# Mixer row projections: two of 512 columns in place of four of 256, with the recurrence's key transposes ahead of the values' projection

## The chip, the cores and the metric

The kernel runs on one core of a Trainium2 chip. The metric is the device time of one execution in microseconds; the time before is 2207.61 us, the median of three runs. Engines are called as in the profile: PE (TensorE), DVE (VectorE), ACT (ScalarE), POOL (GpSimd), SP (SyncE, which here only issues DMAs).

## What is computed

Two blocks follow each other on one sequence of 512 tokens and 1024 channels. The change touches the first, which has two layers, each with a mixer and a feed-forward part. The mixer, cut to what matters here:

```
h = rms_norm(x, attn_norm_w[layer]);  proj = h @ w_in[layer]          # 1024 -> 3072
a_q, a_i, a_zf, a_zb, a_g, b_u, c_q, c_k, c_v = jnp.split(proj, ...)  # 6 x 256, 3 x 512
o_a = hgrn2_mixer(a_q, a_i, a_zf, a_zb, a_g, lb)   # gated recurrence, both directions; a_i: its values
o_b = fourier_mixer(b_u)                           # 2-D DFT, over positions and channels
o_c = dilated_attention_mixer(c_q, c_k, c_v, positions)   # rotary on q and k, then attention
x = x + concatenate([o_a, o_b, o_c]) @ w_out[layer]
x = x + square(relu(rms_norm(x, ...) @ w_up)) @ w_down
```

## The kernel before

All weights are split into a rounded part and a remainder, so one product of a tile takes three matmuls: high by high, low by high, high by low. A **chunk** of weights (128 x 2048 words) comes by a DMA from SP into one of two buffers `raw`; ACT casts each half into `WH` (`act_hi`, the cast), DVE makes the remainder `WL` (`dve_lo`), and that half is a **unit** for PE. Three unit buffers exist. SP issues a load once the chunk two before it is split (`sp_chunk`).

Most projections (`pe_lin`) hold the weights still and stream 512 tokens of `HH`/`HL`; their result has channels on the partitions. Four **row projections** of 256 columns per layer need tokens on the partitions: `a_i` (the recurrence's values), `b_u`, and `c_v` in two halves. `pe_rows` holds 128 tokens still and streams 256 columns of weights. ACT empties each result from PSUM, scaled by the norm (`act_made`).

Each engine's program is written as generators woven by a string of letters. In a mixer `u` is a step of the projections (a quarter of one: `u1` to `u48` here), `c` a step of the recurrence; the strings are `MIX_PE`, `MIX_DVE` and `MIX` (ACT and POOL). An engine executes what it is given in that order. The projections stand in the order gates (two), `a_q`, `a_g`, `a_i`, then `c_q` (two halves), `c_k` (two), `b_u`, `c_v` (two). Steps for the next split are two `u` ahead of a chunk's half: at `u38` the first half of chunk 10 is split, at `u42` that of chunk 11.

The recurrence has eight score levels (l = -1 to 6), two `c` each: PE multiplies keys by queries in 128 x 128 blocks (16 matmuls), DVE merges them. Between levels DVE makes the exponents (`apart`), ACT takes `Exp`, POOL and DVE the scaled keys and queries (`queries`). The level -1 starts after `u16` and every level has three `u`, so **level 6** starts after `u37`. After it, in `rec_pe`, come the **key transposes** (four sets of four blocks of 128 x 128), the state's products, the outputs, a sum and its inverse spread over heads (the inverse's broadcast). The sets of the transposes, like all products of the recurrence, go round three PSUM banks (`REC`), and a bank is taken again when its reader is done:

```
                    b = bank()                 # rec_pe: waits for the reader of three sets ago
                        t = e.tr(b[:, ch * 128:(ch + 1) * 128], x.kl[dr][...], ident)
                    e.act(x.Kt[dr]..., t3(b, 4), ACT.Copy)     # rec_act: reads one set
```

So the fourth set's bank is free once ACT has copied the first set.

Rotary turns `c_q` and `c_k`, eight pieces i of 128 x 512. SP swaps each piece's halves by four DMAs into one of two buffers (`sp_turn`), which may start when piece i-2 is finished; POOL multiplies by the cosine, DVE by the sine (`rot_dve`, step i) and, in the next step, adds (piece i-1 finished). `ROT` sets the steps: step i stands two `u` after step i-1. SP's program has, for each of these four projections, the swaps of its two pieces behind the load of the chunk three later:

```
                sp_chunk(e, n)
                if n - 3 in lin_of_chunk and lin_of_chunk[n - 3] in turned_lins:
                    sp_turn(e, lin_of_chunk[n - 3])
```

Behind the projections stand the DFT (`four_pe`, two parts) and the attention.

Of the kernel before, what the change touches and what calls it, by code (L numbers as in the profile page):

```python
# [12 lines left out]
ACT = mybir.ActivationFunctionType  # L13
# [3 lines left out]
S = 512  # L17
# [32 lines left out]
class Book:  # L50
# [17 lines left out]
    def at(self, name, *key):  # L68

        return (self.handle(name), 0) if self.counting else (self.handles[name], self.values[name, key])  # L70
# [150 lines left out]
def build(nc, I, out):  # L221
    ctx = ExitStack()
    with ctx:
# [61 lines left out]
        rcol = small[:, 232:236]  # L285
# [19 lines left out]
        def lin(src, kind, to=None, j=0, ly=0):  # L305
            lins.append(Lin(len(lins), [chunk(x) for x in src], kind, to, j, ly))
            return lins[-1]
# [4 lines left out]
        def unit(u):  # L312
            cs = slice(u % NUNIT * UNIT, (u % NUNIT + 1) * UNIT)
            return WH[:, cs], WL[:, cs]
# [6 lines left out]
        def mix_memory(ly):  # L321
            m = Mix()
# [36 lines left out]
            m.ms, m.rs, m.ris = (small[:, 256 + 32 * i:288 + 32 * i] for i in range(3))  # L359
            W = I["w_in"][ly]  # L360
            m.head = [lin([W[2, 0]], "gate", j=0, ly=ly), lin([W[3, 0]], "gate", j=1, ly=ly),
                      lin([W[0, 0]], "silu", m.aq2, ly=ly), lin([W[4, 0]], "silu", m.ag2, ly=ly),
                      lin([W[1, 0]], "rows", m.ai3, ly=ly)]
            m.tail = [lin([W[6 + j, 0]], "copy", m.cq3[:, 2 * j:2 * j + 2], ly=ly) for j in range(2)]
            m.tail += [lin([W[8 + j, 0]], "copy", m.ck3[:, 2 * j:2 * j + 2], ly=ly) for j in range(2)]
            m.tail += [lin([W[5, 0]], "rows", m.u3, ly=ly)]
            m.tail += [lin([W[10 + j, 0]], "rows", m.cv3[:, :, 256 * j:256 * j + 256], ly=ly) for j in range(2)]
            m.dft = chunk(I["dft"], "raw")
            m.out = [lin([I["w_out"][ly][j, 0]], "res", (m.scratch, 2 * ly), j, ly) for j in range(4)]
            f = m.ffn = Mix()  # L370
# [127 lines left out]

        BANK, BEFORE, holder = {}, {}, {}
        for l in lins:  # L500
            for m in range(2):
                b = (2 * (l.n - s2.low[0].n) + m) % 3 if l.kind in ("lat", "shift", "keep") else l.n % 2 * 2 + m
                BANK[l.n, m], BEFORE[l.n, m] = b, holder.get(b)
                holder[b] = (l, m)

        def bank_of(l, m):
            return bk(BANK[l.n, m])

        def clear(e, l, m):

            if BEFORE[l.n, m]:
                e.wait_ge(*emptied(*BEFORE[l.n, m]))

        def emptied(l, m):

            return at("lin_act" if l.kind in ("rows", "copy") else "lin_dve", "ps", l.n, m)
# [23 lines left out]
        def pe_lin(e, l):  # L540
            for ci, n in enumerate(l.chunks):
                u0 = chunks[n][2]
                for h in range(2):
# [4 lines left out]
                    for m in range(2):  # L548
# [15 lines left out]
                            t.then_inc(*did("w_use", u))  # L564
                        yield

        def pe_rows(e, l):

            u0 = chunks[l.chunks[0]][2]
            for h in range(2):  # L570
                e.wait_ge(*at("w_lo", u0 + h))
                wh, wl = unit(u0 + h)
                for m in range(2):
                    if h == 0:
                        clear(e, l, m)
                    for tk in (2 * m, 2 * m + 1):
                        o = bank_of(l, m)[:, tk % 2 * 256:(tk % 2 + 1) * 256]
                        for k in range(4):
                            xh, xl, made = operand(l, h * 4 + k)
                            e.wait_ge(*at(*made))  # L580
                            xh, xl = xh[:, tk * 128:(tk + 1) * 128], xl[:, tk * 128:(tk + 1) * 128]
                            ws = slice(k * 256, (k + 1) * 256)
                            e.mm(o, xh, wh[:, ws], h + k + tk % 2 == 0, False)
                            e.mm(o, xl, wh[:, ws], False, False)
                            t = e.mm(o, xh, wl[:, ws], False, h + k + tk % 2 == 5)
                    if h:
                        t.then_inc(*did("lin_mm", l.n, m))
                    elif m:
                        t.then_inc(*did("w_use", u0))
                    yield  # L590

        def pe_lins(e, ls):
            for l in ls:
# [1 line left out]

        def act_made(e, l):

            for m in range(2):
                ps = bank_of(l, m)
                if l.kind in ("gate", "silu"):  # L600
                    sg = mixes[l.ly].sg[m]
                    e.wait_ge(*at("lin_dve", "ps", l.n, m))
                    if l.kind == "silu":
                        p = lins[l.n - 1]
                        e.wait_ge(*at("lin_dve", "sg" if p.kind == "gate" else "out", p.n, m))
                    e.act(sg, sg if l.kind == "gate" else l.to[:, m, :], ACT.Sigmoid).then_inc(*did("lin_act", "sg", l.n, m))
                elif l.kind == "rows":
                    e.wait_ge(*at("lin_mm", l.n, m))
                    e.wait_ge(*at("nrm_dve", 2 * l.ly - 1, "col"))
                    for i in range(2):  # L610
                        t = e.act(l.to[:, 2 * m + i, :], ps[:, i * 256:(i + 1) * 256], ACT.Copy,
                                  rcol[:, 2 * m + i:2 * m + i + 1])
                    t.then_inc(*did("lin_act", "ps", l.n, m))
                elif l.kind == "copy":
                    e.wait_ge(*at("lin_mm", l.n, m))
                    e.act(l.to[:, m, :], ps, ACT.Copy).then_inc(*did("lin_act", "ps", l.n, m))
                elif l.kind == "keep":
                    e.wait_ge(*at("lin_dve", "ps", l.n, m))
                    e.act(s2.keep[m], s2.keep[m], ACT.Sigmoid).then_inc(*did("lin_act", "keep", l.n, m))
                elif l.kind == "hid":  # L620
                    f, half = l.to
                    t = 2 * l.j + m
                    e.wait_ge(*at("ffn_dve", l.ly, half, "sq", t))
                    e.act(f.hh[:, t, :], f.rl[m], ACT.Copy).then_inc(*did("ffn_act", l.ly, half, "hi", t))
                elif l.kind == "res" and l.to[1] is not None:
                    act_next(e, l, m)
# [281 lines left out]
        def rec_pe(e, x):  # L908
# [32 lines left out]
                        t = e.tr(b[:, ch * 128:(ch + 1) * 128], x.kl[dr][:, (hp * 4 + ch) * 128:(hp * 4 + ch + 1) * 128], ident)  # L941
                    t.then_inc(*did("rec_pe", ly, "kt", dr, hp))
            yield
            e.wait_ge(*at("lin_act", "ps", x.head[4].n, 1))
            for dr in range(2):
                for hp in range(2):
                    e.wait_ge(*at("rec_act", ly, "kt", dr, hp))
# [268 lines left out]
        def four_pe(e, x, first_scores):  # L1216
            ly = x.ly
            n = x.dft
            e.wait_ge(*at(f"raw{n % NRAW}", n))
            e.wait_ge(*at("fou_dve", ly, "folded"))  # L1220
            for part in range(2):
                w = slot(n)[:, part * 768:(part + 1) * 768]
                for d in range(2):
                    b, ds = bk(part * 2 + d), slice(d * 128, (d + 1) * 128)
                    l = x.tail[-1 if part else -2]
                    e.wait_ge(*emptied(l, 1))
                    e.wait_ge(*emptied(x.tail[-1], 1))
                    e.mm(b[:, 0:128], x.u04[:, ds], w[:, 0:128])
                    e.mm(b[:, 256:384], x.u24[:, ds], w[:, 128:256])
                    for k in range(2):  # L1230
                        t = e.mm(t3(b, 2)[:, :, 128:256], x.uo[:, k, ds], t3(w[:, 256 + k * 256:512 + k * 256], 2), k == 0, k == 1)
                    if part and d:
                        t.then_inc(*did("raw_use", n))
                        mark("raw_use", ly, part, d)
                    else:
                        t.then_inc(*did("raw_use", ly, part, d))
                yield
            e.wait_ge(*at("fou_act", ly, 0, 1))
            next(first_scores)
            for d in range(2):  # L1240
                e.wait_ge(*at("fou_act", ly, 1, d))
                e.mm(bk(2 + d), c("cd"), x.us[d], True, False)
                e.mm(bk(2 + d), c("sd"), x.us[2 + d], False, True).then_inc(*did("fou_pe", ly, d))
            yield
# [26 lines left out]

        ROT = 14

        def turned_of(x, i):

# [196 lines left out]
        def win_dve(e, x):  # L1474
# [17 lines left out]
            for i in range(9):  # L1492
                steps[f"s{ROT + i}"] = lambda i=i: rot_dve(e, x, i)
            for i, also in ((21, fold), (22, fold_again)):
                steps[f"s{i}"] = lambda i=i, also=also: (rot_dve(e, x, i - ROT), also(e, x))
            yield from between(dve_lins(e, x.head + x.tail, True), **steps)
            att = att_dve(e, x.ly, x, full, mask, -0.125, evac)
            yield from four_dve(e, x, att)
# [5 lines left out]
        def win_pool(e, x):  # L1504
            yield from between(range(48), **{f"s{ROT + i}": lambda i=i: rot_pool(e, x, i) for i in range(8)})

        MIX = "u" * 12 + "c" + "uu" + "cucuu" * 8 + "cuu" * 4 + "cuuuc"
        MIX_DVE = "u" * 12 + "c" + "uu" + "cuucu" * 8 + "cuu" * 4 + "cuuuc"
        MIX_PE = "u" * 16 + "c" + "cucuu" * 8 + "cu" * 2 + "cuuu" + "cu" + "cuuuc"

# [1765 lines left out]
def layout(inp):  # L3278
# [6 lines left out]
    a["w_out"] = np.stack([lay(g["w_out"][i], 8, 256) for i in range(2)])  # L3285
    a["w_up"] = np.stack([lay(g["w_up"][i], 8, 256) for i in range(2)])
    a["w_down"] = np.stack([lay(g["w_down"][i], 8, 256) for i in range(2)])
    q = {k[:-2]: x[0] for k, x in g.items() if k.endswith("_2")}
    a["pos2"] = np.ascontiguousarray(g["positions_2"][0])
    w = q["w_in"]  # L3290
# [43 lines left out]
```

## Time and profile before

| What | Value |
|---|---|
| timed runs | 2207.59, 2207.61, 2208.95 us |
| span of the profiled execution | 2211.8 us |
| PE busy | 2148.4 us, 97% of the span |
| DVE / ACT / POOL busy | 1324.7 / 949.9 / 189.1 us |
| chain that ended last | PE 86%, DVE 7%, ACT 3% |
| first mixer's projections and recurrence | 10 to 193 us |
| the same part of the second | begins 639 us later |

The span is what the profiler saw from the first to the last instruction of one execution; a time of its own beside the span was not kept for it. It is 4.2 us above the median of the timed runs, so a difference worked out from its rows is put on the median.

### The profile page before, as it was taken

The page shows a single profiled execution, that of the slowest core. Times are in us where ns is not written, and L with a number is a line of the kernel's source. Part 1 is how long each engine was busy: PE and PEld are TensorE (multiplying, and loading weights), DVE is VectorE, ACT ScalarE, POOL GpSimd, SP SyncE. Part 2 cuts the span into 40 slices and gives each one's busy share as a digit, 9 for nine tenths or more (in the row PEclk, how much of TensorE's full clock was granted, in tenths as well). Part 3 has the DMA queues.
Part 4 walks back from the last instruction along what each step waited for, and adds up shares of the span by engine and source line. Part 5 has one row for each costly group of instructions (what it writes and reads, how often), then busy time and mean ns, then how long its engine had stood idle before and what let it go on. Part 6 is the DMA issues. An engine that isn't in the chain of part 4 may idle for free.

```text
span 2211.8 us, 32932 instructions
## 1 busy us (share of the span) xinstructions
PE 2148.4 (97%) x13984; PEld 1681.6 (76%) x13984; DVE 1324.7 (60%) x1976; ACT 949.9 (43%) x1442; POOL 189.1 (9%) x159
## 2 busy tenths in 40 slices
PE   8998999999999999999999999999999998999997
PEld 6885688888888785788888885676888567777775
DVE  8886555335437867455255453857433454888887
ACT  5445532222234347432223332345221234888885
POOL 1220000000001310100000200000000001122220
PEclk9999999999999999999999999999999998999999
DMA  5222033322222231222222221212110443799985
GB/s 187 69 80 77 20 119 119 119 101 97 102 85 77 72 96 39 76 83 102 102 96 95 96 96 55 77 53 82 59 59 32 144 168 125 292 349 364 358 346 217
DMA packets 55000, 275.69 MB, mean 125 GB/s; under 512 B 13142, under 2 KB 13398, under 8 KB 26048
## 3 DMA queue, kind: packets, MB, share of 16 engines
q1 hardware_dynamic: 45344, 264.32, 33.0%
q0 software_dynamic: 8928, 8.33, 1.1%
q8 instruction: 113, 1.85, 0.3%
q10 hardware_dynamic: 576, 0.87, 0.1%
q14 instruction: 39, 0.32, 0.0%
HBM read 268.31 MB, written 29.36 MB: 135 GB/s over the span
## 4 chain that ended last, share of the span: by engine, by line
PE 86%; DVE 7%; ACT 3%; DMA 1%; issue 1%; SPq 0%; POOL 0%; POOLq 0%; DVEq 0%; ACTq 0%
PE psum L123 83%; PE psum L126 3%; DVE A_mix L136 2%; ACT A_mix L130 1%; DVE WL L136 1%; DMA A_moe<-h_rows,A_moe 1%; ACT A_mix L133 1%; DVE A_second L136 1%; DVE A_mix L156 0%; DVE A_second L144 0%; DVE A_mix L162 0%; ACT WH L130 0%; SPq L168 0%; DMA A_mix<-A_mix 0%; DVE HL L136 0%
## 5 line engine op out<-in xcount | busy, mean ns | idle before, releaser
L136 DVE TENSOR_TENSOR WL<-raw,WH 128x1024 fp32r<-128x1024 f32 x236 | 300.9, 1277 | 351.6 <-ACT WH L130 351.2
L130 ACT ACTIVATE WH<-raw 128x1024 fp32r<-128x1024 f32 x236 | 247.5, 1054 | 357.6 <-PE psum L123 341.7
L123 PE MATMUL psum<-HH,WH 128*128 128x512 f32 x736 | 301.6, 410 | 17.5 <-DVE HL L144 10.1
L123 PE MATMUL psum<-R_op,WH 128*128 128x512 f32 x1024 | 316.0, 390 | 0.0
L123 PE MATMUL psum<-R_ffn,WH 128*128 128x512 f32 x1024 | 315.1, 389 | 0.0
L123 PE MATMUL psum<-HH,WL 128*128 128x512 f32 x736 | 290.3, 394 | 0.0
L123 PE MATMUL psum<-HL,WH 128*128 128x512 f32 x736 | 290.2, 394 | 0.0
L123 PEld LDWEIGHTS psum<-R_op,WH 128*128 128x128 f32 x1024 | 192.2, 188 | 40.6 <-issue 1.0
L123 PEld LDWEIGHTS psum<-R_ffn,WH 128*128 128x128 f32 x1024 | 192.2, 188 | 39.9
L123 PE MATMUL psum<-R_moe 128*128 128x512 f32 x800 | 198.3, 404 | 5.8 <-DVE ring_moe L136 3.4
L123 PE MATMUL psum<-R_ffn,WL 128*128 128x512 f32 x512 | 199.2, 389 | 0.0
L123 PE MATMUL psum<-R_op,WL 128*128 128x512 f32 x512 | 199.2, 389 | 0.0
L123 PEld LDWEIGHTS psum<-HH,WH 128*128 128x128 f32 x736 | 140.2, 190 | 64.2 <-DVE WL L136 16.5
L123 PEld LDWEIGHTS psum<-R_moe 128*128 128x128 f32 x800 | 151.5, 193 | 39.9 <-DVE ring_moe L136 4.3
L123 PEld LDWEIGHTS psum<-HH,WL 128*128 128x128 f32 x736 | 140.1, 190 | 30.5
L123 PEld LDWEIGHTS psum<-HL,WH 128*128 128x128 f32 x736 | 140.4, 191 | 29.0 <-issue 1.9
L123 PE MATMUL psum<-A_second 64*64 64x64 f32 (+4 forms) x3736 | 154.1, 233 | 4.8 <-DVE A_second L156 1.8
L136 DVE TENSOR_TENSOR R_moe<-ring_moe,R_moe 128x1024 fp32r<-128x1024 f32 x128 | 150.8, 1219 | 9.4 <-ACT R_moe L130 9.3
L123 PEld LDWEIGHTS psum<-A_second 64*64 64x64 f32 (+3 forms) x3736 | 124.3, 137 | 34.7 <-issue 23.5
L130 ACT ACTIVATE R_moe<-ring_moe 128x1024 fp32r<-128x1024 f32 x128 | 135.5, 1063 | 24.4 <-PE psum L123 16.0
L123 PE MATMUL psum<-A_mix 128*64 128x128 f32 (+4 forms) x1408 | 126.4, 316 | 8.1 <-DVE small L162 3.2
L130 ACT ACTIVATE A_second<-psum 128x512 f32<-128x512 f32 (+3 forms) x101 | 48.0, 494 | 190.7 <-PE psum L123 176.8
(206 smaller groups left out, 3000.1 us busy)
## 6 DMA issues: line engine op xcount, KB each, us to landing
ring_moe<-in_w_gu SPq DMA_DIRECT2D x64, 1024.0 KB, 10.1
raw<-in_w_in SPq DMA_DIRECT2D x41, 1024.0 KB, 5.0
raw<-in_w_up SPq DMA_DIRECT2D x32, 1024.0 KB, 4.9
raw<-in_w_down SPq DMA_DIRECT2D x32, 1024.0 KB, 4.9
ring_moe<-in_w_dn SPq DMA_DIRECT2D x32, 1024.0 KB, 6.8
raw<-in_w_out SPq DMA_DIRECT2D x12, 1024.0 KB, 4.9
kept<-A_second SPq DMA_DIRECT2D x20, 256.0 KB, 2.6
A_mix<-A_mix SPq DMA_DIRECT2D x64, 64.0 KB, 2.0
```

Of the source, the lines that this page charges most:

```text
L123: return self.raw.matmul(o, l, r, start=start, stop=stop)
L126: return self.raw.matmul(o, i, ident, is_transpose=True, start=True, stop=True)
L130: return self.raw.activation(o, i, f, scale=scale)
L133: return self.raw.activation(o, i, f, scale=scale, bias=bias, accum_out=accum)
L136: return self.raw.tensor_tensor(o, a, b, op)
```

## The change

The four row projections become two of 512 columns, each from two chunks: A is `a_i` and `b_u` side by side, B is `c_v`. A new array `w_row` holds their weights. In `pe_rows` one matmul now streams 512 columns, and each token tile has a PSUM bank to itself, four a projection. Their last unit takes the token tiles in the order 2, 3, 0, 1 (`ROWS`), and the DFT's first part waits for tile 3 alone. Since `a_i` leaves the head of the list, `c_q` and `c_k` stand at `u17` to `u32` (before: `u21` to `u36`), A at `u33` to `u40`, B at `u41` to `u48`. The rotary's steps follow: `ROT` is 12 in place of 14. PE makes the key transposes behind `u40` (before: behind `u41`) and the state's products behind `u42`, as before. ACT copies the transposed keys behind its `u42` (before: behind `u40`).

```diff
-                      lin([W[0, 0]], "silu", m.aq2, ly=ly), lin([W[4, 0]], "silu", m.ag2, ly=ly),
-                      lin([W[1, 0]], "rows", m.ai3, ly=ly)]
+                      lin([W[0, 0]], "silu", m.aq2, ly=ly), lin([W[4, 0]], "silu", m.ag2, ly=ly)]
...
-            m.tail += [lin([W[5, 0]], "rows", m.u3, ly=ly)]
-            m.tail += [lin([W[10 + j, 0]], "rows", m.cv3[:, :, 256 * j:256 * j + 256], ly=ly) for j in range(2)]
+            for j, to in enumerate(((m.ai3, m.u3), (m.cv3,))):
+                m.tail.append(lin([I["w_row"][ly, j, k] for k in range(2)], "rows", to, ly=ly))
...
+        ROWS = (2, 3, 0, 1)
+            us = [chunks[n][2] + h for n in l.chunks for h in range(2)]
+            for i, u in enumerate(us):
+                e.wait_ge(*at("w_lo", u))
+                wh, wl = unit(u)
+                final = u == us[-1]
+                order = ROWS if final else (0, 1, 2, 3)
+                for tk in order:
+                    if i == 0:
+                        clear(e, l, tk)
+                    o, ts = bank_of(l, tk), slice(tk * 128, (tk + 1) * 128)
+                    for k in range(2):
+                        xh, xl, made = operand(l, 2 * i + k)
+                        e.wait_ge(*at(*made))
+                        ws = slice(k * 512, (k + 1) * 512)
+                        e.mm(o, xh[:, ts], wh[:, ws], i + k == 0, False)
+                        e.mm(o, xl[:, ts], wh[:, ws], False, False)
+                        t = e.mm(o, xh[:, ts], wl[:, ws], False, final and k == 1)
...
+            if l.kind == "rows":
+                e.wait_ge(*at("nrm_dve", 2 * l.ly - 1, "col"))
+                for tk in ROWS:
+                    ps, w = bank_of(l, tk), S // len(l.to)
+                    e.wait_ge(*at("lin_mm", l.n, tk))
+                    for i, to in enumerate(l.to):
+                        t = e.act(to[:, tk, :], ps[:, i * w:(i + 1) * w], ACT.Copy, rcol[:, tk:tk + 1])
...
-            e.wait_ge(*at("lin_act", "ps", x.head[4].n, 1))
+            e.wait_ge(*at("lin_act", "ps", x.tail[4].n, 1))
...
-                    l = x.tail[-1 if part else -2]
-                    e.wait_ge(*emptied(l, 1))
-                    e.wait_ge(*emptied(x.tail[-1], 1))
+                    e.wait_ge(*emptied(x.tail[-1], 1 if part else 3))
...
-        ROT = 14
+        ROT = 12
...
-        MIX = "u" * 12 + "c" + "uu" + "cucuu" * 8 + "cuu" * 4 + "cuuuc"
+        MIX = "u" * 12 + "c" + "uu" + "cucuu" * 8 + "cuuuu" + "cuu" * 2 + "c" + "cuuuc"
...
-        MIX_PE = "u" * 16 + "c" + "cucuu" * 8 + "cu" * 2 + "cuuu" + "cu" + "cuuuc"
+        MIX_PE = "u" * 16 + "c" + "cucuu" * 8 + "cc" + "uu" + "cuuu" + "cu" + "cuuuc"
```

**ACT, behind level 6.** Here `WH<-raw` is a cast, `A_mix<-psum 128x4x128` a copy of a set of transposed keys, and `A_mix<-psum,small` the emptying of a row projection. Before:

```order
L130 ACTIVATE A_mix<-A_mix 128x1024 [waits s_rec_dve] x2
L130 ACTIVATE WH<-raw 128x1024 [waits s_w_use]
L130 ACTIVATE A_mix<-psum 128x4x128 [waits s_rec_pe] x4
L130 ACTIVATE A_mix<-psum,small 128x256 [waits s_lin_mm]
L130 ACTIVATE A_mix<-psum,small 128x256
L130 ACTIVATE A_mix<-psum,small 128x256 [waits s_lin_mm]
L130 ACTIVATE A_mix<-psum,small 128x256
L130 ACTIVATE WH<-raw 128x1024 [waits s_raw1]
L130 ACTIVATE WH<-raw 128x1024 [waits s_w_use]
```

Now:

```order
L130 ACTIVATE A_mix<-A_mix 128x1024 [waits s_rec_dve] x2
L130 ACTIVATE WH<-raw 128x1024 [waits s_w_use]
L130 ACTIVATE A_mix<-psum,small 128x256 [waits s_lin_mm,s_nrm_dve]
L130 ACTIVATE A_mix<-psum,small 128x256
L130 ACTIVATE A_mix<-psum,small 128x256 [waits s_lin_mm]
L130 ACTIVATE A_mix<-psum,small 128x256
L130 ACTIVATE A_mix<-psum,small 128x256 [waits s_lin_mm]
L130 ACTIVATE A_mix<-psum,small 128x256
L130 ACTIVATE A_mix<-psum,small 128x256 [waits s_lin_mm]
L130 ACTIVATE A_mix<-psum,small 128x256
L130 ACTIVATE WH<-raw 128x1024 [waits s_raw1]
L130 ACTIVATE A_mix<-psum 128x4x128 [waits s_rec_pe] x4
```

The cast that waits for `s_raw1`, the landing of chunk 11, stood behind the four key copies and stands ahead of them now, with eight emptyings of A ahead of it.

**PE, the key transposes.** They are the rows `psum<-C,A_mix`; the rows `psum<-WH,HH` are the first matmuls of a unit of a row projection. Before, behind the first quarter of `c_v`'s first half, and the matmul behind them:

```order
L126 MATMUL psum<-C,A_mix 128x128 [waits s_rec_act,s_rec_dve]
L126 MATMUL psum<-C,A_mix 128x128 x3
L126 MATMUL psum<-C,A_mix 128x128 [waits s_rec_act]
L126 MATMUL psum<-C,A_mix 128x128 x3
L126 MATMUL psum<-C,A_mix 128x128 [waits s_rec_act,s_rec_dve]
L126 MATMUL psum<-C,A_mix 128x128 x3
L126 MATMUL psum<-C,A_mix 128x128 [waits s_rec_act]
L126 MATMUL psum<-C,A_mix 128x128 x3
L123 MATMUL psum<-WH,HH 128x256 [waits s_lin_act]
```

Now, behind the last of A and ahead of the first of B:

```order
L123 MATMUL psum<-WL,HH 128x512
L126 MATMUL psum<-C,A_mix 128x128 [waits s_rec_act,s_rec_dve]
L126 MATMUL psum<-C,A_mix 128x128 x3
L126 MATMUL psum<-C,A_mix 128x128 [waits s_rec_act]
L126 MATMUL psum<-C,A_mix 128x128 x3
L126 MATMUL psum<-C,A_mix 128x128 [waits s_rec_act,s_rec_dve]
L126 MATMUL psum<-C,A_mix 128x128 x3
L126 MATMUL psum<-C,A_mix 128x128 [waits s_rec_act]
L126 MATMUL psum<-C,A_mix 128x128 x3
L123 MATMUL psum<-WH,HH 128x512 [waits s_lin_act,s_w_lo]
```

The transposes moved ahead of one quarter of a projection; their waits are the same, and the fourth set's is for ACT.

**SP, the loads of the row projections and the swaps.** `A_mix<-A_mix` are swaps, `raw<-in_w_in` and `raw<-in_w_row` loads of chunks. Before, from the swaps of `c_k`'s first half to the DFT's table (the load in it is chunk 11):

```order
L168 DMA A_mix<-A_mix 32x512 [waits s_rot_dve,s_lin_act]
L168 DMA A_mix<-A_mix 32x512 x3
L168 DMA A_mix<-A_mix 32x512 [waits s_rot_dve,s_lin_act]
L168 DMA A_mix<-A_mix 32x512 x3
L168 DMA raw<-in_w_in 128x2048 [waits s_w_lo]
L168 DMA A_mix<-A_mix 32x512 [waits s_rot_dve,s_lin_act]
L168 DMA A_mix<-A_mix 32x512 x3
L168 DMA A_mix<-A_mix 32x512 [waits s_rot_dve,s_lin_act]
L168 DMA A_mix<-A_mix 32x512 x3
L168 DMA raw<-in_dft 128x1536 [waits s_w_lo]
```

Now, from the load of chunk 10 to the DFT's table, chunk 11 the second load in it:

```order
L168 DMA raw<-in_w_row 128x2048 [waits s_w_lo]
L168 DMA A_mix<-A_mix 32x512 [waits s_rot_dve,s_lin_act]
L168 DMA A_mix<-A_mix 32x512 x3
L168 DMA A_mix<-A_mix 32x512 [waits s_rot_dve,s_lin_act]
L168 DMA A_mix<-A_mix 32x512 x3
L168 DMA raw<-in_w_row 128x2048 [waits s_w_lo]
L168 DMA raw<-in_dft 128x1536 [waits s_w_lo]
```

The load of chunk 11 stood behind the swaps of piece 5 and stands behind those of piece 7 now, the last of the rotary.

## Rows read from the trace of the kernel before

**Rows 1.** The page: span, busy time of the engines, chain that ended last.
```profile
span 2211.8 us, 32932 instructions
PE 2148.4 (97%) x13984; PEld 1681.6 (76%) x13984; DVE 1324.7 (60%) x1976; ACT 949.9 (43%) x1442; POOL 189.1 (9%) x159
PE 86%; DVE 7%; ACT 3%; DMA 1%; issue 1%; SPq 0%; POOL 0%; POOLq 0%; DVEq 0%; ACTq 0%
```

**Rows 2.** Waits of PE, 59 to 193 us: us in total, times, longest.
```profile
PE psum L123 <- ACT A_mix L130: 1.0, 1, 1.0
PE psum L123 <- DVE A_mix L144: 0.7, 1, 0.7
```

**Rows 3.** Timeline, PE: start, duration; two steps of either kind of projection, and what follows.
```profile
65.18 0.39 PE L123 MATMUL psum<-WH,HH 128*128 128x256 f32 x1
...
71.13 1.16 PE L123 MATMUL psum<-A_mix 64*128 64x128 f32 x16
...
88.59 0.50 PE L123 MATMUL psum<-HH,WH 128*128 128x512 f32 x1
...
94.26 1.16 PE L123 MATMUL psum<-A_mix 64*128 64x128 f32 x16
```

**Rows 4.** Timeline, PE, level 6 in the first layer and the step behind it.
```profile
138.02 1.16 PE L123 MATMUL psum<-A_mix 64*128 64x128 f32 x16 [0.34 <-DVE A_mix L136]
...
142.18 1.16 PE L123 MATMUL psum<-A_mix 64*128 64x128 f32 x16
143.27 0.39 PE L123 MATMUL psum<-WH,HH 128*128 128x256 f32 x1
```

**Rows 5.** Timeline, all engines, 151 to 162 us (SPq is the issue of DMAs).
```profile
150.61 0.68 DVE L136 TENSOR_TENSOR A_mix<-A_mix 128x512 f32<-128x512 f32 x1
...
151.36 3.10 SPq L168 DMA_DIRECT2D A_mix<-A_mix  x4
152.00 1.94 PE L126 MATMUL psum<-C,A_mix 128*128 128x128 f32 x16
152.64 2.07 ACT L130 ACTIVATE A_mix<-psum 128x512 f32<-128x512 f32 x4 [2.32 <-PE psum L126]
...
154.56 1.59 ACT L130 ACTIVATE A_mix<-psum,small 128x256 f32<-128x256 f32 x4
...
159.64 2.01 ACT L130 ACTIVATE WH<-raw 128x1024 fp32r<-128x1024 f32 x2 [3.49 <-DMA raw<-in_w_in]
```

**Rows 6.** Timeline, SP, the issue of chunk 9's load.
```profile
109.25 0.33 SPq L168 DMA_DIRECT2D raw<-in_w_in  x1
```

**Rows 7.** Timeline, ACT: level 6's copies and the cast of chunk 9's second half; a later cast.
```profile
139.18 1.56 ACT L130 ACTIVATE A_mix<-psum 64x256 f32<-64x256 f32 x4 [6.83 <-PE psum L123]
140.76 1.06 ACT L130 ACTIVATE WH<-raw 128x1024 fp32r<-128x1024 f32 x1
...
149.26 1.06 ACT L130 ACTIVATE WH<-raw 128x1024 fp32r<-128x1024 f32 x1
```

**Rows 8.** Timeline, PE, the start of level 6 in the second layer.
```profile
777.17 1.16 PE L123 MATMUL psum<-A_mix 64*128 64x128 f32 x16 [0.34 <-DVE A_mix L136]
```

**Rows 9.** Timeline, ACT, the casts of chunk 11 in the second layer.
```profile
798.02 2.01 ACT L130 ACTIVATE WH<-raw 128x1024 fp32r<-128x1024 f32 x2 [2.73 <-DMA raw<-in_w_in]
```

**Rows 10.** Timeline, PE, the first matmul behind a wait, in the second block.
```profile
1521.18 0.80 PE L123 MATMUL psum<-HH,WH 128*128 128x512 f32 x1 [2.86 <-DVE A_second L136]
```

**Rows 11.** Windows there: length, busy us of PE, PEld, DVE, ACT, POOL, granted clock, DMA.
```profile
1521.00:1527.00 6.00, 5.82 (x14) 4.58 (x15) 4.32 (x6) 4.91 (x7) 0.00 (x0) 0.50 0.23 87
1527.00:1533.00 6.00, 6.00 (x28) 4.93 (x27) 5.07 (x9) 5.48 (x5) 0.31 (x1) 0.98 0.47 165
```

**Rows 12.** Timeline, DVE, levels 4 and 5 of the first layer.
```profile
117.05 1.39 DVE L156 COPY_PREDICATED A_mix<-M,psum 128x512 f32<-128x512 uint8 x2 [1.53 <-PE psum L123]
...
120.39 1.76 DVE L136 TENSOR_TENSOR A_mix<-A_mix 128x512 f32<-128x512 f32 x1
...
132.38 1.85 DVE L136 TENSOR_TENSOR WL<-raw,WH 128x1024 fp32r<-128x1024 f32 x1 [1.76 <-ACT WH L130]
```

More of the change, by code:

```diff
@@ L500, in build @@
         for l in lins:
-            for m in range(2):
-                b = (2 * (l.n - s2.low[0].n) + m) % 3 if l.kind in ("lat", "shift", "keep") else l.n % 2 * 2 + m
+            for m in range(4 if l.kind == "rows" else 2):
+                b = (2 * (l.n - s2.low[0].n) + m) % 3 if l.kind in ("lat", "shift", "keep") else (l.n % 2 * 2 + m) % 4
                 BANK[l.n, m], BEFORE[l.n, m] = b, holder.get(b)
@@ L565, in pe_lin @@
                         yield
+        ROWS = (2, 3, 0, 1)
         def pe_rows(e, l):
[L569 to L590, printed above, removed]
@@ new lines, in pe_rows @@
+            us = [chunks[n][2] + h for n in l.chunks for h in range(2)]
[15 more added lines that the diff above has]
+                        t = e.mm(o, xh[:, ts], wl[:, ws], False, final and k == 1)
+                    if final:
+                        t.then_inc(*did("lin_mm", l.n, tk))
+                    elif tk == 3:
+                        t.then_inc(*did("w_use", u))
+                    if tk in (order[1], order[3]):
+                        yield
@@ L596, in act_made @@
         def act_made(e, l):
+            if l.kind == "rows":
[5 more added lines that the diff above has]
+                        t = e.act(to[:, tk, :], ps[:, i * w:(i + 1) * w], ACT.Copy, rcol[:, tk:tk + 1])
+                    t.then_inc(*did("lin_act", "ps", l.n, tk))
+                return
             for m in range(2):
@@ L606, in act_made @@
                     e.act(sg, sg if l.kind == "gate" else l.to[:, m, :], ACT.Sigmoid).then_inc(*did("lin_act", "sg", l.n, m))
[L607 to L613, printed above, removed]
                 elif l.kind == "copy":
@@ L1494, in win_dve @@
             for i, also in ((21, fold), (22, fold_again)):
-                steps[f"s{i}"] = lambda i=i, also=also: (rot_dve(e, x, i - ROT), also(e, x))
+                steps[f"s{i}"] = lambda also=also: also(e, x)
             yield from between(dve_lins(e, x.head + x.tail, True), **steps)
@@ L3287, in layout @@
     a["w_down"] = np.stack([lay(g["w_down"][i], 8, 256) for i in range(2)])
+    a["w_row"] = np.stack([lay(np.concatenate([w[:, 256:512], w[:, 1280:1536], w[:, 2560:3072]], 1), 4, 512)
+                           for w in (g["w_in"][i] for i in range(2))])
     q = {k[:-2]: x[0] for k, x in g.items() if k.endswith("_2")}
```

## The prediction

> **What bounds the kernel now.** I read the page first: PE is busy for 97% of the span and makes 86% of the chain that ended last [rows 1]. So the time is PE's work plus the few places where PE waits. Next I read who PE waits for in the first mixer. Between 59 and 193 us the reader is to see short waits only: 1.0 us for ACT (the DFT's first part, which waits for the emptying of the last row projection), 0.7 for the recurrence's state on DVE [rows 2]; a third, 0.34 at the start of level 6 for the queries on DVE, stands in PE's timeline [rows 4]. Then I read timelines around what the diff touches: PE's steps [rows 3], and all engines at the key transposes [rows 5]. There ACT copies the keys as soon as PE has turned them, empties a row projection, and then sits idle for 3.49 us before a cast, until chunk 11 has landed. Nobody minds that idle time before. The second mixer repeats the first, 639 us later [rows 4, 8]. I work out one layer and then the second by its own rows.
>
> **What is removed: 384 matmuls of 256 columns become 192 of 512.** A pair of steps of the old kind lasts from 65.18 to 71.13, 5.95 us; a pair of 512-column steps from 88.59 to 94.26, 5.67 us [rows 3]. The second is a projection with the weights held still; a row projection of 512 columns streams as many columns through as many held ones, so I take its price. That is 0.14 us a step. Of 16 such steps a layer, five stand ahead of level 6 (0.7 us) and eleven behind its start (1.5 us). The Trainium skill ("TensorE: Matmul & The Clock Gate", section "Back-to-back issue gap") gives a warm start-to-start of N/2.4 GHz + 2.5 ns; an estimate by it is 109.2 ns at 256 and 215.8 ns at 512 columns, so 384 and 192 matmuls differ by 0.5 us a layer in place of 2.2, and my sum below would end 3.4 us higher, at 2232. The trace does not agree: with what lies between, 5.95/48 = 124 and 5.67/24 = 236 ns [rows 3]. The rows decide.
>
> **What the transposes' place costs.** This is the term that sets the sign, so I follow it instruction by instruction, counted from the start of level 6 on PE (138.02) [rows 4].
>
> PE first. Before, it reached the transposes at 152.00 [rows 5], 13.98 us after level 6 began. The stretch holds both parts of level 6, one single step and three steps in a row; the three ran from 143.27 to 152.00, 8.73 us [rows 4, 5]. Now only a pair stands there, 5.67 us [rows 3], and the single step loses 0.14. So PE is at the transposes 13.98 - 3.06 - 0.14 = 10.8 us after level 6 begins. Sixteen took 1.94 us with the last one's drain [rows 5], so the fourth set is due at 10.8 + 1.3 = 12.1.
>
> The fourth set takes the bank of the first and needs ACT's copy of it. Before, that copy started 0.64 us after the first transpose [rows 5], in time. Now ACT has two things ahead of it: the eight emptyings of A and the cast of chunk 11's first half, and that cast needs the load. The load's chain is the same as before, only other pieces of the rotary stand in it. Before: DVE's step at `u38` (rotary step 4) finished piece 3 at 150.61 + 0.68 = 151.29; SP issued piece 5's four swaps from 151.36 for 3.10 us, then the load; the cast began at 159.64 [rows 5]. Now rotary step 6 stands at the same `u38`, finishes piece 5, SP issues piece 7's swaps and then the load. Everything up to there hangs on level 6, as before: DVE's `u38` stands behind the two parts of level 6 in its program. So the cast starts 159.64 - 138.02 = 21.6 us after level 6 begins, lasts 1.06 [rows 7], the first copy takes 2.07/4 = 0.5 [rows 5], and PE's fourth set may start at 23.2. **PE stands still for 23.2 - 12.1 = 11.1 us.** In the second layer the cast began 798.02 - 777.17 = 20.85 us after level 6 [rows 8, 9], so 22.4 - 12.1 = **10.3 us**. Queued behind the fourth set are the whole of B, the state's products, the outputs and the DFT; nothing on PE can go ahead.
>
> Behind a wait the clock is lower. At 1521.18 PE had waited 2.86 us [rows 10], and from 1521 to 1527 the granted clock was 0.50 (1.2 GHz), then 0.98 again; 14 matmuls of 512 columns fitted into the 6 us, against 28 in the next 6 [rows 11]. So a long wait costs up to about 2.9 us more; less if the transposes right behind it let part of it pass. I take 2.5 each, with 0 and 2.9 as the bounds.
>
> **What is given back.** With PE 10 us late, the state on DVE (0.7) is ready long before the outputs. The DFT's first part waits for tile 3, emptied while PE does tiles 0 and 1, which saves 1.0 [rows 2]. Both are gone: -1.7 a layer. Emptying in four pieces of 512 and the key copies themselves are ACT's work under PE's cover: if the cover went, the four tiles would cost about as much as the last emptyings do now, 1.0. The new wait for `b_u` and `a_i` together is covered, since A's emptying is ahead of the key copies on ACT.
>
> **What the earlier rotary costs in the levels.** Ahead of level 6 DVE now has rotary steps 0 to 4 where it had 0 to 2: four more operations of 0.68 us [rows 5], up to 1.76 where one took longest [rows 12]. DVE was already late at level 6, by 0.34 [rows 4]. Its own idle time, 1.53 at 117.05 and 1.76 at 132.38 [rows 12], can take some of it. The bounds are -0.7 (all absorbed, and PE's five cheaper steps come through) and +3.5 (four at 1.76, half absorbed); I take +0.7, as most of 2.7 us fits into 3.3 us of idle time, of which the part that waits on ACT moves along. It delays level 6 and everything behind it alike, so it adds to the stall and does not replace it.
>
> **The sum.** First layer: 11.1 + 2.5 - 1.7 - 1.5 + 0.7 = +11.1. Second: 10.3 + 2.5 - 1.7 - 1.5 + 0.7 = +10.3. Together +21.4 us. The rows come from an execution whose span is 2211.8, 4.2 us above the median of the timed runs; as a difference it goes on the median: 2207.6 + 21.4 = **2229 us**. With the bounds of the clock (0 to 2.9) and of the levels (-0.7 to 2, beyond which I count it a rival) it runs from 2221 to 2232.
>
> **The rivals.** *The load is early.* If chunk 11 lands 5 us sooner than before, the cast does not wait, but ACT still has its program: the last cast ahead ended at 149.26 + 1.06 = 150.3, 12.3 after level 6 [rows 7]; eight emptyings take 2 x 1.59 = 3.2, the cast 1.06, the first copy 0.5 [rows 5, 7], and the fourth set goes at 17.1. The wait is 5.0 us, a layer loses 5.0 + 2.5 - 1.7 - 1.5 + 0.7 = 5.0, and the time is 2217.6. For it: SP's four swaps took 3.10, which one queue with less in it could do faster. Against it: the finished piece that starts the chain stands at the same `u38`.
>
> *DVE falls behind.* Rotary operations take 1.76 instead of 0.68 [rows 5, 12], the levels lose 3.5 each layer instead of 0.7, and the time is 2229 + 5.6 = 2235. Against it: the other such operation shown takes 0.68.
>
> *Faster.* If the key copies go ahead of the waiting cast, the fourth set starts on time and there is no long wait: -1.7 - 1.5 + 0.7 = -2.5 a layer, 2202.6 us. It decides at 12.1 us after level 6: a first copy done by then, and the change is a gain. Against it stands a row: chunk 9 was issued at 109.25 [rows 6], yet ACT cast its second half at 140.76, after 6.83 us of idle time that ended with level 6's copies, which stand ahead of it in ACT's program [rows 7]. An instruction that was ready did not pass one that waited. The Trainium skill says the same of ACT and DVE ("PSUM — Partial Sum Buffer", section "Engine vs sequencer instructions": "strict FIFO"); by that rule alone this rival had no chance, and the row agrees with it, with 6.83 us.
>
> **How the numbers follow.** The forecast has 0.76, the early load 0.09, DVE behind 0.08, faster 0.05; 0.02 stay for other ways near no change. A measurement of this kernel can tell about 0.2%, 4.4 us. Slower by more than that are the first three, and I give 0.91; faster 0.05; within it 0.04. The range reaches from the early load, 2217, to DVE behind, 2235, and holds the time 8 times in 10.
>
> **What would show it.** In the profile after: a wait of PE of 10 to 11 us for ACT at the key transposes, before their last set, in either layer; ahead of it ACT idle before `WH<-raw` until a DMA of `w_row`; a granted clock near 0.5 right behind; no wait of 0.7 for the state and of 1.0 for the DFT; 512-column row matmuls some 0.23 us apart. If the key copies start within a microsecond of the transposes, my reading of ACT's order is wrong and so is the sign. If the wait is there but near 5 us, the load came early. If level 6 starts more than 3 us late, the levels were underpriced.

## The result and the profile after

The changed kernel takes 2251.2 us, the median of four runs (2248.78 to 2252.36), against 2208.28 us for the kernel before (2207.59 to 2211.77, four runs beside them). The ratio is 1.0186 (95%: 1.0172 to 1.0201): slower by 1.9%, some 43 us. The forecast was 2229 with a range to 2235. The sign was right; the loss is twice what I gave.

The page of the changed kernel, as in [rows 1]:

```profile
span 2249.4 us, 32154 instructions
PE 2142.7 (95%) x13600; PEld 1658.5 (74%) x13600; DVE 1320.5 (59%) x1976; ACT 949.7 (42%) x1434; POOL 189.1 (8%) x159
```

PE has 384 matmuls fewer and is busy for 5.7 us less, in a longer span. So the time is in waits and what follows from them, and the waits of PE in the first mixer (60 to 215 us) say for whom, beside [rows 2]:

```profile
PE psum L126 <- ACT A_mix L130: 10.3, 1, 10.3
PE psum L123 <- ACT A_mix L130: 9.0, 2, 8.4
PE psum L123 <- DVE WL L136: 2.5, 2, 1.5
```

The first wait is the one that I predicted, at the key transposes. The second, of 8.4 us, I had not. The rest of these rows is mostly old: 0.59 of the 9.0 us stands in the attention, and 1.46 of the 2.5 at 77.67, where the kernel before waits 1.34 us for `WL` too, a wait that [rows 2] and the prediction left out. New is 1.07 us for `WL` at 122.05. PE's timeline shows their places (start, duration, in brackets the idle time ahead):

```profile
60.21 1.16 PE L123 MATMUL psum<-A_mix 64*128 64x128 f32 x16
...
122.05 0.50 PE L123 MATMUL psum<-WH,HH 128*128 128x512 f32 x1 [1.07 <-DVE WL L136]
...
124.70 0.39 PE L123 MATMUL psum<-WL,HH 128*128 128x512 f32 x1
133.50 0.80 PE L123 MATMUL psum<-WH,HH 128*128 128x512 f32 x1 [8.42 <-ACT A_mix L130]
...
138.89 1.16 PE L123 MATMUL psum<-A_mix 64*128 64x128 f32 x16
...
144.00 0.50 PE L123 MATMUL psum<-WH,HH 128*128 128x512 f32 x1
...
149.67 1.16 PE L123 MATMUL psum<-A_mix 64*128 64x128 f32 x16
...
160.40 1.47 PE L126 MATMUL psum<-C,A_mix 128*128 128x128 f32 x12
172.16 1.12 PE L126 MATMUL psum<-C,A_mix 128*128 128x128 f32 x4 [10.29 <-ACT A_mix L130]
172.92 0.78 PE L123 MATMUL psum<-WH,HH 128*128 128x512 f32 x1
...
180.14 1.04 PE L123 MATMUL psum<-A_mix 128*64 128x64 f32 x28
...
209.07 1.13 PE L123 MATMUL psum<-A_mix,C 32*128 32x512 f32 x4
```

The row of 122.05 is A's first step, `u33`. Its unit takes the token tiles 0, 1, 2, 3, six matmuls each. PE does two tiles and stops at the third for 8.42 us. Level 6 begins at 149.67, where it was at 138.02 [rows 4]: 11.65 us late, before the predicted wait has begun. That one follows 10.29 us long at the last set of transposes. The last row is the inverse's broadcast, behind everything that the change touches; the kernel before has it at 188.49.

The windows around the two waits (length, busy us of PE, PEld, DVE, ACT, POOL, granted clock, DMA) show what each leaves behind:

```profile
126.00:133.50 7.50, 0.00 (x0) 0.00 (x0) 5.54 (x7) 2.65 (x4) 3.29 (x3) 0.67 0.59 185
133.50:139.40 5.90, 5.89 (x20) 4.32 (x22) 0.00 (x0) 1.39 (x2) 2.15 (x2) 0.55 0.00 0
139.40:145.00 5.60, 5.60 (x44) 4.46 (x43) 4.55 (x7) 0.00 (x0) 0.00 (x0) 1.00 0.01 2
161.80:172.00 10.20, 0.07 (x1) 0.00 (x0) 7.27 (x8) 4.25 (x10) 1.71 (x1) 0.71 0.60 206
172.00:178.00 6.00, 5.84 (x19) 4.88 (x20) 1.47 (x2) 1.68 (x4) 0.00 (x0) 0.64 0.00 0
178.00:184.00 6.00, 6.00 (x68) 4.91 (x67) 2.75 (x11) 1.06 (x1) 0.00 (x0) 1.00 0.01 3
```

Behind the first wait A's pair of steps lasts 16.84 us in all (122.05 to 138.89): 8.42 of wait, 5.67 of work at full clock, and 2.75 for a clock near 0.5. Behind the second, B's first pair lasts 7.22 (172.92 to 180.14), 1.55 more than at full clock. In the second mixer the same two cost 1.96 and 1.01 us.

Who holds PE up stands in ACT's timeline:

```profile
130.71 2.26 ACT L130 ACTIVATE A_mix<-A_mix 128x1024 f32<-128x1024 f32 x2 [9.68 <-DVE A_mix L136]
132.87 1.07 ACT L130 ACTIVATE A_mix<-psum 128x512 f32<-128x512 f32 x2
...
160.51 1.04 ACT L130 ACTIVATE WH<-raw 128x1024 fp32r<-128x1024 f32 x1
161.58 3.03 ACT L130 ACTIVATE A_mix<-psum,small 128x256 f32<-128x256 f32 x8
170.56 1.06 ACT L130 ACTIVATE WH<-raw 128x1024 fp32r<-128x1024 f32 x1 [5.95 <-DMA raw<-in_w_row]
171.52 1.55 ACT L130 ACTIVATE A_mix<-psum 128x512 f32<-128x512 f32 x3
```

The row of 132.87 empties the last half of `c_k`. Each copy reads one of the two banks that A wants for its tiles 2 and 3; PE goes on 0.63 us after the first begins. The copies stand behind two exponentials, for which ACT waits 9.68 us on DVE. The last four rows are the predicted wait: cast, eight emptyings, 5.95 us idle until chunk 11 has landed, the cast, and only then the key copies.

The first two stood in that order in ACT's timeline of before too:

```profile
128.16 2.27 ACT L130 ACTIVATE A_mix<-A_mix 128x1024 f32<-128x1024 f32 x2 [8.68 <-DVE A_mix L136]
130.33 1.06 ACT L130 ACTIVATE A_mix<-psum 128x512 f32<-128x512 f32 x2
```

PE stood still for neither then [rows 2]: the projection behind `c_k` was `b_u`, which took the two banks of `c_k`'s first half, and `c_k`'s last half kept its own until `c_v`.

The second mixer does the same: waits of 8.43 and 10.50 us. From the first score level to the inverse's broadcast, the mixers of the changed kernel take 148.86 and 147.81 us (60.21 to 209.07, 717.26 to 865.07), those of before 128.54 and 128.55 (59.95 to 188.49, 699.11 to 827.66): +20.3 and +19.3. Together that is 39.6 us, within the 38 to 44 of the timed ratio's interval.

### The profile page after: what moved, and what is told of

Its sections match the earlier page's. It is cut to its first block, busy times and chain, and to the rows that moved or that the text cites. A ratio compares the mean times of both kernels' runs of the same rounds, so it can differ in the third digit from the quotient of the medians.

```text
span 2249.4 us, 32154 instructions
## 1 busy us (share of the span) xinstructions
PE 2142.7 (95%) x13600; PEld 1658.5 (74%) x13600; DVE 1320.5 (59%) x1976; ACT 949.7 (42%) x1434; POOL 189.1 (8%) x159
## 4 chain that ended last, share of the span: by engine, by line
PE 86%; DVE 6%; ACT 4%; DMA 2%; issue 1%; SPq 0%; POOL 0%; DVEq 0%; POOLq 0%; ACTq 0%
PE psum L123 83%; PE psum L126 3%; DVE A_mix L136 2%; ACT A_mix L130 1%; DMA A_moe<-h_rows,A_moe 1%; ACT WH L130 1%; DVE A_second L136 1%; DVE WL L136 1%; ACT A_mix L133 1%; DVE A_second L144 0%; DMA raw<-in_w_row 0%; DVE A_mix L162 0%; SPq L168 0%; ACT branch_gates L133 0%; DVE A_mix L156 0%
## 5 line engine op out<-in xcount | busy, mean ns | idle before, releaser
L123 PE MATMUL psum<-HH,WH 128*128 128x512 f32 x736 | 299.9, 407 | 17.6 <-DVE HL L144 9.9
```

What stands on the lines that cost most here:

```text
L123: return self.raw.matmul(o, l, r, start=start, stop=stop)
```

## The experiments

**Theories.** Theory 1: there are two waits of PE, each made by a place in ACT's program: the key copies behind the cast of chunk 11, and the emptying of `c_k`'s last half behind level 6's exponentials. Each costs its wait and the low clock behind it. Rivals: chunk 11's load is late and ACT's order matters little; or the earlier rotary makes DVE late, and ACT with it. All edits are against the changed kernel. The first four ran beside a kernel before of 2208.9 us, the last four beside one of 2209.23.

**Key copies first.** ACT's string has its old end again:

```diff
-        MIX = "u" * 12 + "c" + "uu" + "cucuu" * 8 + "cuuuu" + "cuu" * 2 + "c" + "cuuuc"
+        MIX = "u" * 12 + "c" + "uu" + "cucuu" * 8 + "cuu" * 4 + "cuuuc"
```

> The string for ACT is put back, so that ACT copies the transposed keys ahead of the emptying of A and ahead of the cast of chunk 11. Theory 1 (each of PE's two long waits comes from the place of one piece of work in ACT's program): only the second wait goes, 10.3 us a layer in the first and 10.5 in the second; with some 1.5 us of low clock behind each, less up to 1.5 for B's first tile, which now waits for A's emptying behind the key copies: about 20 us less, 2230 us. The wait ahead of level 5 (8.4 us) stays. Rival (the loads are late, whatever ACT's order): the wait moves to the units of chunk 11 and the time stays near 2251.

Measured: 2232.03 us, ratio 1.0101 (1.0085 to 1.0116). PE's timeline:

```profile
133.16 0.80 PE L123 MATMUL psum<-WH,HH 128*128 128x512 f32 x1 [8.41 <-ACT A_mix L130]
...
161.71 0.66 PE L126 MATMUL psum<-C,A_mix 128*128 128x128 f32 x4 [0.36 <-ACT A_mix L130]
164.00 0.47 PE L123 MATMUL psum<-WH,HH 128*128 128x512 f32 x1 [1.62 <-ACT A_mix L130]
```

The wait of 10.3 us is gone with ACT's order alone, though chunk 11 comes no earlier; the other stays. A short wait of 1.62 us is new: A's emptying now stands behind the key copies, and B's first tile wants a bank of A's.

**Empty `c_k` earlier.** ACT empties the last half of `c_k` at its `u32`, ahead of the exponentials, and not at `u34`:

```diff
-            yield from between(act_lins(e, x.head + x.tail, True), **steps)
+            def made(e, l):
+                if l not in (x.tail[3],):
+                    act_made(e, l)
+
+            steps["s15"] = lambda: act_made(e, x.tail[3])
+            yield from between(side_lins(e, x.head + x.tail, made, act_hi, True), **steps)
```

> ACT empties the last key projection right behind its step u32 instead of at u34, ahead of level 5's exponentials instead of behind them. Theory 1: A's third tile finds its bank empty, the wait of 8.4 us and the 2.7 us of low clock behind it go in either layer, about 22 us less, 2229 us; the second wait (10.3) stays. Rival (DVE is late because the rotary steps stand earlier, and the bank only shows it): PE goes on to level 5 and waits there about as long for the queries, and less than 6 us are won in all.

Measured: 2233.56 us, ratio 1.0114 (1.0096 to 1.0131). PE's timeline:

```profile
121.09 0.50 PE L123 MATMUL psum<-WH,HH 128*128 128x512 f32 x1 [1.07 <-DVE WL L136]
131.64 1.16 PE L123 MATMUL psum<-A_mix 64*128 64x128 f32 x16 [0.75 <-DVE A_mix L156]
139.46 1.16 PE L123 MATMUL psum<-A_mix 64*128 64x128 f32 x16 [0.95 <-DVE A_mix L136]
...
161.79 1.12 PE L126 MATMUL psum<-C,A_mix 128*128 128x128 f32 x4 [10.16 <-ACT A_mix L130]
```

The mirror image: the first wait is gone, the second stays. (The exponentials are level 6's, as in the theory above; the expectation calls them level 5's.) What the first one covered is seen now: besides the 1.07 us at `u33`, two more waits for DVE, of 0.75 us in level 5 and 0.95 at level 6. So 17.6 us are won and not 22.

**Both edits.**

> Both edits: keys first on ACT, and the last key projection emptied at u32. Theory 1: both waits go and what the prediction gave the change without them is left: 16 cheaper steps (-2.2 a layer), the two short waits (-1.7), against DVE's later level 6 (+0.7) and B's first tile behind the key copies (+1.3): 2207 us, within 3 us of the kernel before. Rival (late loads or a late DVE): over 2215 us.

Measured: 2211.23 us, ratio 1.0015 (1.0006 to 1.0024). Against the changed kernel the edits give 19.2 and 17.6 us alone, 36.8 in sum, and 40.0 together. With intervals of 2 to 4 us on each time they add up, and nearly the whole loss is theirs. The time is above the 2207 that I gave with its 3 us; my own terms add up to less still, -1.9 a layer, some 2205. Timeline of PE, and a window:

```profile
140.39 1.16 PE L123 MATMUL psum<-A_mix 64*128 64x128 f32 x16 [0.95 <-DVE A_mix L136]
...
152.91 0.66 PE L126 MATMUL psum<-C,A_mix 128*128 128x128 f32 x4 [0.34 <-ACT A_mix L130]
155.19 0.47 PE L123 MATMUL psum<-WH,HH 128*128 128x512 f32 x1 [1.62 <-ACT A_mix L130]
```

```profile
155.20:159.00 3.80, 3.80 (x10) 3.03 (x11) 1.45 (x2) 2.03 (x6) 1.34 (x1) 0.57 0.68 177
```

What is left: level 6 is 2.4 us later than before (140.39 against 138.02), and in the first mixer the clock falls to 0.57 behind the wait for B's first tile. In the second it does not (last section).

**Load chunk 11 early.** SP issues its load ahead of the swaps of pieces 6 and 7; ACT keeps the changed order:

```diff
+            ahead = [x.tail[5].chunks[1] for x in mixes]
...
-                sp_chunk(e, n)
+                if n not in ahead:
+                    sp_chunk(e, n)
+                if n + 1 in ahead:
+                    sp_chunk(e, n + 1)
```

> Only the load of chunk 11 is moved, ahead of the swaps of pieces 6 and 7 on SP. Theory 1, with the early load as the prediction priced it: the cast does not wait, but ACT still empties A and casts ahead of the key copies, so the second wait falls from 10.3 to about 5 us, some 10 us less in all, 2241 us. If the place of the key copies behind the cast did not matter, the time would stay at 2251; if the load alone mattered, the wait would be gone, 2230.

Measured: 2237.36 us, ratio 1.0128 (1.0113 to 1.0144). PE's timeline:

```profile
134.46 0.79 PE L123 MATMUL psum<-WH,HH 128*128 128x512 f32 x1 [8.53 <-ACT A_mix L130]
...
167.06 1.12 PE L126 MATMUL psum<-C,A_mix 128*128 128x128 f32 x4 [4.22 <-ACT A_mix L130]
```

With the load out of the way the key copies still come 4.2 us late, behind ACT's emptyings and cast. My rival "the load is early" gave 5.0 us for this case. So the load makes some 6 us of the second wait and ACT's order the rest; the rival that the load alone counts falls. The time is 13.8 us less than the changed kernel's, where I expected some 10.

**Empty A in halves.** Both edits above, and ACT empties A's tiles 2 and 3 at `u40`, ahead of the key copies, and 0 and 1 at `u42`, behind them; the recurrence's last two exponentials go behind both:

```diff
+                if l is x.tail[4]:
+                    act_made(e, l, ROWS[2:])
+                    e.wait_ge(*at("rec_dve", x.ly, "kl", 0))
+                    e.act(x.E8[0], shifted(x, 0), ACT.Exp).then_inc(*did("rec_act", x.ly, "qe", 0))
...
+            steps["s19"] = lambda: act_made(e, x.tail[4], ROWS[:2])
```

> On top of both edits, ACT empties A in two halves: tiles 2 and 3 ahead of the key copies, tiles 0 and 1 behind them, and the last two exponentials of the recurrence go behind both. In the kernel with both edits PE still waits 1.6 us for B's first tile behind the key transposes, and the window behind it shows a granted clock of 0.57, which costs a pair of steps 7.25 in place of 5.67 us. Theory 1 (place in ACT's program, and the clock falls with the wait): both go, 0.3 + 1.6 + 1.6 a layer, 7 us less than with both edits, 2204 us. Rival (the clock falls because of the key transposes themselves, not of the wait): only 1.9 a layer go, 2207 us, and the window keeps its low clock.

Measured: 2206.33 us, ratio 0.9985 (0.9976 to 0.9993). PE's waits at the transposes and at B's first tile are gone in both mixers; level 6 is still late for DVE:

```profile
141.16 1.16 PE L123 MATMUL psum<-A_mix 64*128 64x128 f32 x16 [0.98 <-DVE A_mix L136]
...
151.91 1.94 PE L126 MATMUL psum<-C,A_mix 128*128 128x128 f32 x16
```

The time lies between the 2204 of the theory and the 2207 of the rival. The clock is full behind the transposes (1.00 from 153.60 to 157.60), so the rival's sign is not there. But with both edits alone it was low in one of the two mixers only, so the test says little on what lowers it, and there was less to win than I had put down.

**Rotary back.** Both edits above, and the rotary's steps and swaps stand four `u` later, where they were before the change:

```diff
-        ROT = 12
+        ROT = 14
...
-                steps[f"s{i}"] = lambda also=also: also(e, x)
+                steps[f"s{i}"] = lambda i=i, also=also: (rot_dve(e, x, i - ROT), also(e, x))
...
-                if n - 3 in lin_of_chunk and lin_of_chunk[n - 3] in turned_lins:
-                    sp_turn(e, lin_of_chunk[n - 3])
+                if n - 4 in lin_of_chunk and lin_of_chunk[n - 4] in turned_lins:
+                    sp_turn(e, lin_of_chunk[n - 4])
```

> On top of both edits, the rotary's steps go back to where they stood before (14 in place of 12, each projection's swaps one load later on SP), so DVE's levels hold what they held before. Theory 1 (the rotary's earlier place delays DVE, which is why level 6 starts 2.4 us later than before and PE waits 1.07, 0.75 and 0.95 us for DVE): these waits go and level 6 starts at or ahead of 138 us; 2 to 3 us a layer, 2206 us. Rival (DVE is late for another reason, such as PE's different steps): level 6 stays at 140.4 and the time at 2211.

Measured: 2205.4 us, ratio 0.9984 (0.9975 to 0.9993). PE's timeline, and the window behind its last row:

```profile
138.63 1.16 PE L123 MATMUL psum<-A_mix 64*128 64x128 f32 x16 [0.32 <-DVE A_mix L136]
...
153.44 0.47 PE L123 MATMUL psum<-WH,HH 128*128 128x512 f32 x1 [1.63 <-ACT A_mix L130]
```

```profile
153.40:157.00 3.60, 3.56 (x16) 2.95 (x17) 1.21 (x2) 2.10 (x6) 1.10 (x1) 1.00 0.57 149
```

Level 6 waits for DVE as it did before the change, 0.32 us [rows 4], and the waits of 1.07 and 0.75 us are gone, so the theory holds. Level 6 comes at 138.63 and not by 138, as this execution had lost some 2 us before 84 us; in the second mixer it comes 77.54 us after the first score level, against 78.06 before. The same wait for B's first tile stands there as with both edits, yet the clock stays at 1.00.

**Both of these together.** Halves and rotary back, on both edits.

> Both edits, A emptied in halves, and the rotary back at its old place. If the waits are all that the change costs and the cheaper steps all that it brings, the rest is 16 x 0.14 + 1.7 a layer less than before, less what stays of short waits: about 2201 us, faster than the kernel before by 0.3%. If the cheaper steps are lost in waits for DVE, it stays at 2208.

Measured: 2205.7 us, ratio 0.9981 (0.9971 to 0.9992): 3.5 us faster than before, less than I expected. PE's timeline:

```profile
137.25 1.16 PE L123 MATMUL psum<-A_mix 64*128 64x128 f32 x16 [0.32 <-DVE A_mix L136]
...
147.96 1.94 PE L126 MATMUL psum<-C,A_mix 128*128 128x128 f32 x16
...
165.92 6.82 PE L123 MATMUL psum<-A_mix 128*64 128x128 f32 x80 [0.61 <-DVE A_mix L144]
...
184.90 1.13 PE L123 MATMUL psum<-A_mix,C 32*128 32x512 f32 x4
```

The mixers take 125.17 and 126.00 us from the first score level to the broadcast (59.73 to 184.90, 694.17 to 820.17), 3.4 and 2.5 less than before, where I expected 3.9 each. What is missing is the wait for the state, which is back: 0.61 us at 165.92 and 1.36 in the second mixer. The timed gain for both mixers has an interval of 1.8 to 6.4 us, so the time does not tell this kernel from the ones with either edit alone (2206.33 and 2205.4).

**Rotary back alone.** The rotary's edit on the changed kernel, ACT's order and emptyings as changed.

> The changed kernel with only the rotary put back to its old place. Theory 1 (both long waits come from places in ACT's program): the waits stay; the first gets about 2 us shorter, since DVE makes level 6's exponents earlier and ACT empties behind them; some 5 us less in all, 2246 us. Rival (the earlier rotary is behind the long waits, by a late DVE and by the load of chunk 11 behind the last swaps): both shrink to a few microseconds, under 2220 us.

Measured: 2245.14 us, ratio 1.0158 (1.0143 to 1.0172). PE's timeline:

```profile
130.35 0.80 PE L123 MATMUL psum<-WH,HH 128*128 128x512 f32 x1 [6.94 <-ACT A_mix L130]
...
168.45 1.12 PE L126 MATMUL psum<-C,A_mix 128*128 128x128 f32 x4 [10.29 <-ACT A_mix L130]
```

Both waits stay, the first 1.5 us shorter. The rival that the earlier rotary is the cause falls; it is worth 6 us of the 43.

## Why the sign was right and the size was not

**The step that failed** is the term "What the earlier rotary costs in the levels", the only one for what delays level 6: +0.7 us in the sum, +11.65 measured (second layer: +10.6 from the first score level on). It priced DVE's added work, and a wait of PE for PSUM banks stood in no term: it was put at nothing without a reason. I priced what ACT does with A, and not what it must do before PE can begin A. The diff's "each token tile has a PSUM bank to itself, four a projection" got no price at all. A takes four banks, two of them full of `c_k`'s last half. [rows 7] and [rows 12] were read for casts and DVE's idle time; the emptying, at 130.33, stands ahead of [rows 7] and was not looked for. (The sentence "The new wait for `b_u` and `a_i` together is covered" is about A's results, and held: PE does not wait for them.) The term is in fact 8.42 of wait, 2.75 of low clock and 1.07 of waiting for `WL`, less 0.6 of cheaper steps. Emptying early removes the wait and its low clock, 21.6 us in both layers; the time falls by 17.6, as shorter waits for DVE then show. The loss that is left, 24.7 us, is near the forecast's 21.4.

**The transposes' place** was right, and near in size: 10.29 and 10.50 us where I had 11.1 and 10.3, from the chain that I described (level 6, DVE, swaps, load, cast). The cast came 20.9 us after level 6 in the first layer, for 21.6. The key copies moved on ACT remove it. The Trainium skill ("PSUM — Partial Sum Buffer", section "Engine vs sequencer instructions") gives the reason for both waits in two words, "strict FIFO". By it, a copy that is ready is held behind one that is not; the trace agrees, with 9.68 us at 130.71 and 5.95 at 170.56.

**The clock behind that wait** I took as 2.5; it was 1.55 in the first layer and 1.01 in the second. At the first wait it was 2.75 and 1.96, in a term where I had none.

**The 512-column matmuls** are as priced: the pair from 144.00 lasts 5.67 us, as the row of 88.59 had it [rows 3]. That is a gain, seen only when little waits: with the halves and the rotary back together, the mixers are 3.4 and 2.5 us shorter than before, of which 1.0 each is the DFT's wait. The formula that the prediction takes from the Trainium skill ("TensorE: Matmul & The Clock Gate", section "Back-to-back issue gap") is given there for an isolated matmul. Here every matmul has a weight load of its own (13600 of either), so the 236 ns do not test it.

**The two small waits** of [rows 2] are gone, as expected: no wait for the state, and none of 1.0 us for the DFT's first part.

**From level 6 to the broadcast** my terms gave +11.1 + 2.5 - 1.7 - 1.5 = +10.4 us; the trace has 59.40 us for 50.47, +8.9. So this half of the sum held to 1.5 us, and the missing half is all ahead of level 6.

**DVE behind** was a rival at 3.5 us a layer. With PE's first wait gone, level 6 is 2.4 us late and waits for DVE, so DVE is behind indeed; 0.7 was too little. It is not what cost the 43 us.

**Faster** was priced at -2.5 us a layer. With both edits the key copies go first and no long wait is left, and the kernel is still 2.3 us slower than before: level 6 is late, and B's first tile waits for A's emptying, which now stands behind the copies.

**My own sign of failure** did see it: "If level 6 starts more than 3 us late, the levels were underpriced." I had put 0.08 on ways to lose more, none of them on this.

## What to carry to other kernels

When a projection takes more PSUM banks than before, name for each bank who read it last and where that reader stands in its engine's program: here a copy of 0.6 us, behind exponentials that waited for DVE, held PE for 8.4 us and cost the clock behind it. A moved piece of work is priced by everything that then stands ahead of each release on that engine, a load that it waits for included. Where such a change loses, look for the two or three places that hold others up before dropping it: with ACT's two mended the loss of 43 us is 2, and with A emptied in halves, the rotary back, or both, it is a gain of 3 to 4.

## What the chip showed that I had not expected

The clock does not follow the last wait alone. In three kernels (key copies first, both edits, rotary back) PE waits 1.62 or 1.63 us for B's first tile in either mixer. In four of these six places the pair of steps behind it lasts 5.65 or 5.66 us, at full clock. In two it lasts 7.25 and 7.23: the first mixer with both edits (clock 0.57 at first) and the second with the key copies first (from 810.06). With both edits PE had waited 0.75 and 0.95 us for DVE some 23 and 15 us earlier, but so it had in the second mixer, where the pair from this row on takes 5.65:

```profile
794.49 0.47 PE L123 MATMUL psum<-WH,HH 128*128 128x512 f32 x1 [1.62 <-ACT A_mix L130]
```

So these waits do not decide it, and the runs leave open what does.

In the attention behind the mixer, where PE waits 1.40 and 1.06 us in both kernels, the profiled execution of before had a lower clock in the first mixer and that of after had not:

```profile
195.00:215.00 20.00, 16.78 (x101) 8.82 (x101) 14.42 (x44) 14.25 (x33) 0.00 (x0) 0.91 0.23 86
```

```profile
215.00:235.00 20.00, 16.09 (x108) 8.60 (x106) 14.89 (x45) 14.74 (x34) 0.00 (x0) 1.00 0.26 96
```

In the same execution of after, the second mixer's attention had 0.91 (871.50 to 891.50). From the first broadcast to the second mixer's first score level it is 510.62 us before, 508.19 after, 509.27 with the halves and the rotary back together, and 508.16 to 508.20 in the other seven experiments, with no edit in that stretch. Whether one kernel varies so from one execution to the next, a single trace of each cannot tell. A gain of a few us is read from the mixers' own rows rather than from two spans, and even there some 2 us can be lost ahead of every edit, as in the first mixer with the rotary back.
